# Products of constants in TensorE's waits, in a one-core decoder layer with a 32-expert MoE

## The reference, cut to what matters

```
h = rms_norm(x) * (1 + scale1) + shift1
proj = h @ w_in                     # q,k,v of 12 dilated heads and 8 stick-breaking heads, two gates
y = (sigmoid(ga) * (dilated @ w_branch_a) + sigmoid(gb) * (stick @ w_branch_b)) @ w_out
x = x + gate1 * rms_norm(y)
h = rms_norm(x) * (1 + scale2) + shift2
logits = h @ w_router + b_router    # top 4 of 32, softmax over the four
y = sum over the chosen experts of weight * (clamped_swiglu(h @ w_up[e] + b_up[e]) @ w_down[e] + b_down[e])
x = x + gate2 * rms_norm(y)
```

## Time and profile before

| | us |
|---|---|
| median of 3 runs | 1328.16 (1327.51 to 1329.42) |
| the profiled execution | 1325.43 |
| its span, first to last instruction | 1323.3 |
| TensorE busy | 1149.0 (87%) |
| mean granted clock of TensorE | 0.951 |
| DMA, mean over the span | 351 GB/s |

### The profile page before, as it was taken

The page is one execution under the profiler, slowest core; times in us unless marked ns, Lnnn a source line. Parts: engine busy times, 40 slices in busy tenths (PEclk is TensorE's granted clock), DMA queues, the critical chain, the costliest instruction groups (busy, mean ns, idle before and its releaser), DMA issues.

```text
span 1323.3 us, 21402 instructions
## 1 busy us (share of the span) xinstructions
PE 1149.0 (87%) x7951; PEld 575.1 (43%) x7952; DVE 311.8 (24%) x802; ACT 258.4 (20%) x395; POOL 0.2 (0%) x4
## 2 busy tenths in 40 slices
PE   5999899988999779988988989979988778777785
PEld 3744688734344334443343433443433234333232
DVE  2035445274122110211121211212111112111112
ACT  3035422123021111012021111111121111111102
POOL 0000000000000000000000000000000000000000
PEclk9999899997999879989999989989989899899898
DMA  9952665453899999559999999999999999999996
GB/s 349 380 185 96 226 224 217 164 230 149 319 365 416 417 419 418 216 213 418 417 418 417 417 417 417 419 417 419 417 419 417 418 417 417 417 418 418 418 419 278
DMA packets 102526, 464.89 MB, mean 351 GB/s; under 512 B 8188, under 2 KB 9556, under 8 KB 69590
## 3 DMA queue, kind: packets, MB, share of 16 engines
q1 hardware_dynamic: 100112, 460.47, 86.8%
q10 hardware_dynamic: 2374, 3.84, 0.8%
HBM read 463.24 MB, written 1.05 MB: 351 GB/s over the span
## 4 chain that ended last, share of the span: by engine, by line
PE 60%; DMA 24%; SPq 9%; DVE 3%; issue 3%; DVEq 0%; ACT 0%; ACTq 0%
DMA ring<-in_w_up 18%; PE psum L983 18%; PE psum L599 16%; PE psum L1060 9%; PE psum L913 6%; SPq L557 5%; DMA ring<-in_w_down 5%; SPq L552 4%; PE psum L975 2%; PE psum L1078 2%; PE psum L671 1%; DMA ring<-in_ada_w 1%; PE psum L605 1%; DVE area L1756 1%; PE psum L958 1%
## 5 line engine op out<-in xcount | busy, mean ns | idle before, releaser
L983 PE MATMUL psum<-ring,area 128*32 128x512 f32 (+2 forms) x2432 | 401.8, 638 | 66.8 <-DMA ring<-in_w_up 66.5
L983 PEld LDWEIGHTS psum<-ring,area 128*32 128x32 f32 (+2 forms) x2432 | 106.2, 123 | 354.0 <-issue 226.0
L1060 PE MATMUL psum<-ring,area 128*32 128x256 f32 (+2 forms) x2080 | 193.6, 420 | 29.5 <-DVE area L1741 14.8
L913 PEld LDWEIGHTS psum<-area 128*128 128x128 f32 x1056 | 130.1, 204 | 31.9 <-issue 31.9
L913 PE MATMUL psum<-area 128*128 128x128 f32 x1056 | 136.6, 290 | 0.3 <-DVE area L1647 0.3
L1060 PEld LDWEIGHTS psum<-ring,area 128*32 128x32 f32 (+2 forms) x2080 | 75.2, 115 | 137.4 <-issue 66.3
L1716 DVE TENSOR_SCALAR area<-psum 128x256 f32<-128x256 f32 x51 | 21.7, 425 | 408.9 <-PE psum L983 408.9
L1269 ACT ACT_TABLE_LOAD x32 | 41.1, 1283 | 321.7 <-PE psum L958 321.7
L1281 ACT ACTIVATE area<-area 128x256 f32<-128x256 f32 x51 | 21.2, 417 | 422.5 <-DVE area L1716 422.5
L599 PE MATMUL psum<-ring,hT 128*128 128x512 f32 (+1 forms) x192 | 77.5, 559 | 0.0
L1078 PE MATMUL psum<-area 32*128 32x256 f32 (+2 forms) x608 | 55.3, 405 | 18.8 <-DVE area L1756 18.8
(11 more groups left out here) (201 smaller groups left out, 659.3 us busy)
## 6 DMA issues: line engine op xcount, KB each, us to landing
ring<-in_w_up SPq DMA_DIRECT2D x256, 1024.0 KB, 19.5
ring<-in_w_down SPq DMA_DIRECT2D x128, 1024.0 KB, 22.8
ring<-in_ada_w SPq DMA_DIRECT2D x12, 2048.0 KB, 16.7
ring<-in_w_in SPq DMA_DIRECT2D x10, 2048.0 KB, 16.4
ring<-in_w_out SPq DMA_DIRECT2D x2, 2048.0 KB, 10.5
ring<-in_w_in SPq DMA_DIRECT2D x3, 1024.0 KB, 16.1
ring<-in_w_branch_b SPq DMA_DIRECT2D x1, 2048.0 KB, 9.6
cst<-in_cst ACTq DMA_DIRECT2D x1, 1184.5 KB, 8.0
```

The lines of the kernel that those rows point to most:

```text
L913: ins = pe.matmul(ps[banks[i]][:, kk % 4 * P:(kk % 4 + 1) * P], h2[:, tt, kk * P:(kk + 1) * P], S[:, tt, 0:P], start=(tt == 0 and kk % 4 = ...
L983: ins = pe.matmul(ps[b][g * P // G:(g + 1) * P // G, 0:w], XT[:, kk, t0:t0 + P // G], wt[:, c0:c0 + w], start=False, stop=kk == KT - 1, sk ...
L1060: ins = pe.matmul(ps[b][g * M:(g + 1) * M, 0:w], hidT[:, p, q * P + of * M:q * P + (of + 1) * M], down_weights(kk)[:, g * W + d * CW:g * W ...
```

## The change

A helper `keep_busy(b, n, width)` is added to TensorE's program. It issues n products of the 128x128 identity with the identity (width 128) or with 512 columns of constants from its column of ones on (width 512), all written into one PSUM bank that nobody reads. It is called at six places: twice 14 products of 128 columns around the transposing of the small rows; 6 of 128 columns after each `ada_columns`; 2 of 512 columns after `logit_parts(0)`, behind a wait that the bank of "lpart1" is free; 3 of 128 columns before the wait for `sel_ready`; 4 of 128 columns before the wait for `gates_wide`. Nothing is removed or moved, no other engine's program and no DMA differs.

```diff
+            def keep_busy(b, n, width):
+
+                for _ in range(n):
+                    pe.matmul(ps[b][:, 0:width], ident, ident if width == P else cst[:, C_ONE:C_ONE + width],
+                              start=True, stop=True, skip_group_check=True)
+
...
             pe.wait_ge(ld_cst, 16)
+            keep_busy(6, 14, P)
             pe.wait_ge(ld_rows, 96)
             turn("rows", [(bank("rows")[:, 0:R_N], small_rows[:, :], cst[0:R_N, C_ID:C_ID + R_N])])
+            keep_busy(6, 14, P)
             for q in range(4):
...
                 ada_columns(f"ada_a{half}", MOD_A[half])
+                keep_busy(5, 6, P)
                 if half == 0:
                     pe.wait_ge(half_full, 16)
...
             logit_parts(0)
+            un.wait_free(pe, "lpart1")
+            keep_busy(un.bank("lpart1"), 2, CW)
             pe.wait_ge(ada_sum, 8)
...
             turn_back(1)
+            keep_busy(un.bank("acc0"), 3, P)
 
             pe.wait_ge(sel_ready, 1)
...
                           (ps[1][:, 2 * E:3 * E], ones, sel[:, E:2 * E], False, True)])
+            keep_busy(un.bank("acc0"), 4, P)
             pe.wait_ge(gates_wide, 1)
```

## The result

The changed kernel takes 1333.77 us, the median of 22 runs (1324.46 to 1341.16); before, 22 runs beside them, takes 1327.63 us (1325.29 to 1331.68). The ratio of the runs is 1.0038, with a 95% interval of 1.0026 to 1.0051: slower by 5.0 us, 3.5 to 6.8 (the two medians alone lie 6.1 us apart). The forecast was 1323.9 us and faster, with a range of 1321.4 to 1327.4. The runs of the changed kernel also spread over 17 us, where those of before spread over 6.

What follows compares the result with a forecast made beforehand. TensorE's own work up to the expert loop was taken to bound when the weight stream starts. 1.5 (modulation) plus 2.5 (routing) gave 4.0 us, taken as 4.3 against the median: 1328.16 - 4.3 = 1323.9 us, range 1321.4 to 1327.4.

Steps and rivals of the forecast that it cites:

- the first one: Expert loop: a stream of weights that starts when TensorE arrives, so reaching it earlier moves the rest one for one.
- rival 2: Loop: gain given back or absent, as clock falls move or moved code adds a 4.0 us standstill; 1327.9 us, chance 0.11.
- Head: 14 and 14 products around the small rows' transposing: gain 0, since ada2's rows wait for their load at 17.94 us.
- First modulation: 6 and 6 products in TensorE's waits: clock holds in the second half, gain 1.5 us; nothing in the first half.
- Second norm: 2 products of 512 columns behind the router's first products: clock falls all the same, gain 0, upper bound 0.6 to 0.9 us.
- Routing: 3 and 4 products in idle times: gathers at full clock, 3.77 us instead of 6.29, gain 2.5 us.
- Rival 3: Head: products of constants do not raise the clock, ada rows 3.3 us late, modulation adds 1.0; slower, 1332.5 us, chance 0.07.

Runs made afterwards that it cites:

- b3_headnorm: a2_pad15 with only the 28 products of the head and the 2 of 512 columns full size, the others one by one: 1328.03 us, ratio 1.0004.
- c1_again: The unaltered change measured once more, against the kernel before: 1333.0 us, ratio 1.0040.
- c4_pad7: The change plus 7 one-by-one products at the start, 223 instructions more than before: 1330.5 us, ratio 1.0013.
- b1_mod: a2_pad15 with only the 6 and 6 products of the first modulation full size, the others one by one: 1326.54 us, ratio 0.9981.
- a2_pad15: The change plus 15 one-by-one products ahead of its first ones, loop code one whole 16 KB fetch behind that of before: 1324.29 us, ratio 0.9977.
- c3_pad47: The change plus 47 one-by-one products at the start, 383 instructions more than before: 1339.1 us, ratio 1.0075.
- b4_pad31: The change plus 31 one-by-one products at the start, 319 instructions more than before: 1326.1 us, ratio 0.9980.
- b2_route: a2_pad15 with only the 3 and 4 products of the routing full size, the others one by one: 1328.64 us, ratio 1.0002.
- a3_before64: The kernel before plus 64 one-by-one products at the start, 255 instructions more, without the change's products: 1328.44 us, ratio 1.0010.

## Why the prediction was wrong

*The step that failed* is the first one: "whatever makes TensorE reach the loop earlier moves the whole rest earlier, one for one". It did so through expert 5 (3.0 us) and was undone by the loop's own code. The longer program was noticed, as part of rival 2, "the loop's code, moved by 196 instructions, costs TensorE one more standstill such as the 4.03 us at the entry". That was mis-sized twice. A standstill inside the loop, while the weights stream at some 420 GB/s, is 5 to 7 us and not 4, with a stretch of low clock that cost the next 32 MATMULs 2.9 us more; and there were one to five of them, not one. It was also given no case on the slower side. The price should have been bounded from both sides: before shows its own standstill of 4.02 us behind expert 6, at one of its branches and not at the others, so another place of the code could well move or add some.

The Trainium skill, "Runtime: NRT & Kernel Launch", Instruction fetch mechanics, says that a taken branch whose target is outside the fetched window must wait for a fetch by DMA; these runs agree, with up to 7.09 us and one packet of the code queue in each standstill. The same section names 128 KB of instruction memory for TensorE and, a few lines on, only two lines of 16 KB. By the two lines each change to another class would stand, and this the runs do not show: before goes through 31 changes of expert and stands once, for 4.02 us. No run here measures the size.

*Head*: right. 0 was taken, and b3_headnorm with its 0.8 us is within what can be measured. The small rows came 1.2 us late and nobody waited for them. One thing was overlooked: the first rows of ada_w are done earlier, and the load of ada2 lands when it lands (17.43 to 19.51 us), so the wait for it is longer, 1.36 us in the change and 3.72 in c1_again against 0.82, and in c1_again and c4_pad7 ada2's rows then took 3.00 and 3.62 us instead of 1.92.

*First modulation*: right, and undersized. 1.5 us was taken, with up to 1.5 more if the clock falls in the first half too; b1_mod gives 3.8, with 2 either way.

*Second norm*: the clock was expected to fall all the same. It held in the change, in a2_pad15, b3_headnorm and c3_pad47 (eight transposes in 1.09 us), and fell in b4_pad31, c1_again and c4_pad7 (1.63, 1.92 and 1.91 us); the bound of 0.6 to 0.9 us stands.

*Routing*: oversized. 2.5 us was taken for the gathers, and 1.2 to 1.3 is in the traces (5.14 us in the change, 4.99 in b2_route, against 6.29). VectorE's place_ready was checked as the next in line, and the nearer one missed: cls_ready, between the two halves.

*Rival 3* had the right sign for the wrong reason: the products do raise the clock. The sum of the parts, 4.3 us, was right once the code lay as before: a2_pad15 at 1324.29 us, and 4.4 us by ratio against a3_before64. That is luck in part, as the modulation was taken too low and the routing too high.

**The version that beats both** is a2_pad15: faster than before by 3.1 us (1.3 to 4.8). It depends on where the loop's code happens to lie, and any later edit ahead of the loop moves it again.

## What to carry to other kernels

An edit that adds instructions ahead of a loop with rarely taken bodies moves their code. Before the edit's own effect is judged, run it beside a form with as many instructions and no work, and beside one padded by whole fetches; here the place was worth 5 to 13 us (1.0046 against 1.0010, 1.0075 against 0.9977), and the edit 4. In the profile, look for "issue" of several microseconds ahead of a branch target, and for a packet of the code queue within them. Filling a wait with products paid where real work stood behind it at the low clock, and it cost time where the clock was low already and the filling outlasted the wait, as in c1_again.

## What the runs showed of the hardware

A branch with a fetch of code in it cost 3.5 to 4.2 us where few transfers ran (4 to 12 GB/s: at the entry of the loop in all kernels, and behind expert 6 in some) and 5.1 to 7.1 us where the weights streamed (416 to 423 GB/s, the 19 standstills of the table). Code that had been fetched before was fetched again, more often in one execution of a program than in another: 35 and 41 packets for the same instructions.

Products of constants that nobody reads raise the clock: after 28 MATMULs in 5.88 us the next 28 ran in 3.32 us.

What stays open: which rule decides the standstills. Bad were 195, 223 and 383 instructions more, good 0, 255 and 319, so it is neither the length nor a single threshold. A fetch doesn't always mean a standstill either: in before three packets of the code queue start inside expert 9 (624.4, 631.0 and 654.4 us), with 0.82 us ahead of it. Whether the groups of products at the second norm and the routing pay anything by themselves was not resolved either; that would need several times as many runs.
